# Sliding attention's first pairs between the halves of the query chunks, and a split closing of the feed-forward layers

## The reference

```python
def squared_relu_mlp(h, w1, w2):
    a = jax.nn.relu(h @ w1)
    return (a * a) @ w2

def swiglu(x, w_in, w_out):
    gate, up = jnp.split(x @ w_in, 2, axis=-1)
    return (jax.nn.silu(gate) * up) @ w_out

# second layer of the second block (16 query heads, 4 key heads, head size 64, window 128)
q = rotary((hn @ swa_w_q[j]).reshape(B, S, SWA_Q_HEADS, HEAD_DIM), pos)
# sliding_window_sink_attention: per head
s = q @ k.T * 64 ** -0.5, where seen (the last 128 keys)
p = softmax(concatenate([s, sink]))[..., :-1]
o = p @ v
h = h + o.reshape(B, S, ...) @ swa_w_o[j]
h = h + 0.5 * swiglu(rms_norm(h, ffn2_norm), ffn2_w_in, ffn2_w_out)
```

## Time and profile before

| | us |
|---|---|
| median of 3 runs (1851.13 to 1851.97) | 1851.37 |
| the profiled execution's own time | 1850.78 |
| its span | 1849.0 |
| TensorE busy (matmuls) | 1798.1 |
| VectorE busy | 1152.1 |
| ScalarE busy | 859.8 |
| GpSimd busy | 73.4 |

### The profile page before, as it was taken

One profiled execution on the slowest core, in us unless ns is written; L12 is line 12 of the kernel. 1 busy time (PEld: TensorE's weight loads), 2 busy tenths in 40 slices (PEclk: granted clock), 3 DMA queues, 4 the chain that ended last, 5 costly groups with the idle time before them and its releaser, 6 DMA issues.

```text
span 1849.0 us, 26480 instructions
## 1 busy us (share of the span) xinstructions
PE 1798.1 (97%) x10832; PEld 1567.4 (85%) x10835; DVE 1152.1 (62%) x1149; ACT 859.8 (47%) x1046; POOL 73.4 (4%) x118
## 2 busy tenths in 40 slices
PE   9999999999999999999999999999999999899998
PEld 8989988888989878887888898888888887678886
DVE  7665465557556465556666644666666666766665
ACT  6535455555555455545333454533353344454342
POOL 1000000000220000000000011000000000110000
PEclk9999999999999999999999999999999999999999
DMA  9426355556556355555555544555555554336552
GB/s 316 165 69 206 114 183 204 182 181 192 173 167 193 114 169 196 181 182 171 196 180 192 165 136 137 171 189 197 184 173 193 188 180 154 114 115 205 182 182 90
DMA packets 224327, 318.12 MB, mean 172 GB/s; under 512 B 5585, under 2 KB 194145, under 8 KB 224242
## 3 DMA queue, kind: packets, MB, share of 16 engines
q1 hardware_dynamic: 219442, 300.96, 49.1%
q0 software_dynamic: 4800, 15.94, 2.8%
HBM read 315.83 MB, written 1.05 MB: 171 GB/s over the span
## 4 chain that ended last, share of the span: by engine, by line
PE 90%; DVE 5%; ACT 3%; issue 1%; POOL 0%; DMA 0%; SPq 0%; DVEq 0%; ACTq 0%
PE Y L1702 28%; PE C L1640 21%; PE C L1641 11%; PE C L1670 11%; PE Y L1670 8%; PE Y L1611 3%; DVE w_lo L1072 1%; DVE xn L1113 1%; ACT xn L663 1%; ACT w_hi L648 1%; PE C L2108 1%; PE C L1956 1%; PE C L1750 1%; PE C L1864 1%; PE Y L2087 1%
## 5 line engine op out<-in xcount | busy, mean ns | idle before, releaser
L1072 DVE TENSOR_TENSOR w_lo<-raw,w_hi 128x2048 fp32r<-128x2048 f32 x282 | 645.7, 2291 | 337.4 <-ACT w_hi L648 337.0
L648 ACT ACTIVATE w_hi<-raw 128x2048 fp32r<-128x2048 f32 x282 | 538.4, 1910 | 250.7 <-PE Y L1702 170.9
L1640 PE MATMUL C<-at_hl,w_hi 128*128 128x512 f32 x1440 | 511.3, 398 | 0.0
L1641 PE MATMUL C<-at_hl,w_lo 128*128 128x256 f32 x1440 | 404.2, 281 | 0.0
L1640 PEld LDWEIGHTS C<-at_hl,w_hi 128*128 128x128 f32 x1440 | 270.6, 188 | 66.2
L1641 PEld LDWEIGHTS C<-at_hl,w_lo 128*128 128x128 f32 x1440 | 272.0, 189 | 2.1
L1702 PE MATMUL Y<-w_hi,hid_h 128*128 128x512 f32 x656 | 205.0, 394 | 9.6 <-DVE hid_l L1254 3.8
L1702 PE MATMUL Y<-w_lo,hid_h 128*128 128x512 f32 x656 | 203.2, 391 | 0.0
L1702 PE MATMUL Y<-w_hi,hid_l 128*128 128x512 f32 x656 | 202.2, 389 | 0.0
L1702 PEld LDWEIGHTS Y<-w_hi,hid_h 128*128 128x128 f32 x656 | 117.3, 188 | 35.6 <-DVE hid_l L1254 5.5
L1702 PEld LDWEIGHTS Y<-w_lo,hid_h 128*128 128x128 f32 x656 | 123.1, 188 | 27.4
(11 more groups left out here) (285 smaller groups left out, 2430.7 us busy)
## 6 DMA issues: line engine op xcount, KB each, us to landing
raw<-in_ffn_w_in SPq DMA_DIRECT2D x88, 1024.0 KB, 5.1
raw<-in_w_ff SPq DMA_DIRECT2D x64, 1024.0 KB, 5.8
raw<-in_ffn_w_out SPq DMA_DIRECT2D x44, 1024.0 KB, 4.9
raw<-in_w_mem_kv SPq DMA_DIRECT2D x16, 1024.0 KB, 5.3
raw<-in_w_qkv SPq DMA_DIRECT2D x12, 1024.0 KB, 5.3
raw<-in_sb_w_qkv SPq DMA_DIRECT2D x12, 1024.0 KB, 5.1
raw<-in_w_in_ab SPq DMA_DIRECT2D x8, 1024.0 KB, 10.7
raw<-in_w_mem_q SPq DMA_DIRECT2D x8, 1024.0 KB, 5.4
```

Of the source, the lines that this page charges most:

```text
L648: nc.scalar.activation(w_hi[:, n % RING, :], raw[:, n % RAW, :], ACT.Copy).then_inc(hi_split, 1)
L1072: V.tensor_tensor(w_lo[:, n % RING, :], raw[:, n % RAW, :], w_hi[:, n % RING, :].bitcast(f32), ALU.subtract).then_inc(lo_split, 1)
L1640: mm(tiles(to, 2), wh[:, k, part], hl[:, k, :, :], start=k == 0, stop=False)
L1641: last = mm(to[:, S:2 * S], wl[:, k, part], hl[:, k, 0, :], start=False, stop=k == KT - 1)
```

## The change

Four things.

1. On TensorE the scores of pairs 0 to 4, the transposes of pairs 0 to 2 and the contexts of pair 0 move into `q_cols`, between halves of the query chunks. The chunks go to banks 0 and 1 of `Y` in turn, and so do the turns, so that `C` is free for scores and transposes. In `pairs`, iteration i is scores i, transposes i-2, contexts i-4 (it was i-3).
2. On VectorE `q_cols` has both splits of weight chunks first, then rotations, maxima, shares and copies of the first pairs; in `pairs` the copies stand ahead of the shares of the next pair, the low halves of contexts come one iteration later, and the split of the second output chunk moves from `q_cols` to behind the last copies.
3. On ScalarE the exponentials of pairs 0 to 3 move ahead of the copies of query chunks 2 and 3, and the splits of the first output chunks come earlier.
4. In both feed-forward layers the closing is split: of the last but one `down`, block 1 goes in two halves of 6 matmuls, one ahead of the wait for the last hidden columns and one behind block 0 of the last `down`.

```diff
@@ ScalarE
+            def q_cols_(to, at):
+                n = at.chunk
+                for i in range(4):
+                    if i >= 2:
+                        exps("swa", 2 * i - 4, at)
+                        if i == 3:
+                            exps("swa", 3, at)
+                    else:
+                        hi(n + i + AHEAD)
+                    if i == 2:
+                        exps("swa", 1, at)
+                    act.wait_ge(chunk_done, n + i + 1)
+                    nc.scalar.activation(to[i], tiles(Y[:, i % 2, :], 2), ACT.Copy).then_inc(cols_copied, 1)
+                    if 1 <= i <= 2:
+                        hi(n + i + 1 + AHEAD)
@@ VectorE
             def pairs(at):
-                for i in range(PAIRS + 4):
+                for i in range(4, PAIRS + 5):
                     if i < PAIRS:
                         maxima("swa", i, at, score_bank)
-                    if 1 <= i <= PAIRS:
+                    if i < PAIRS + 2:
+                        probs_out(i - 2, at)
+                    if i == 4:
+                        rope_(qT, 3, at.rot - 4, 1)
+                    elif i <= PAIRS:
                         shares("swa", i - 1, at)
-                    if 2 <= i < PAIRS + 2:
-                        probs_out(i - 2, at)
-                    if i >= 4:
-                        contexts(i - 4, at, "swa")
+                    if i == PAIRS + 1:
+                        lo(at.chunk - 1 + AHEAD)
+                    if i >= 5:
+                        contexts(i - 5, at, "swa")
...
-            def q_cols_(n, at):
-                for i in range(n):
-                    lo(at.chunk + i + AHEAD)
-                    if i >= 1:
-                        rope_(qT, i - 1, at.rot)
-                rope_(qT, n - 1, at.rot)
+            def q_cols_(at):
+                n = at.chunk
                 dve.wait_ge(sink_ready, 1)
+                lo(n + AHEAD)
+                lo(n + 1 + AHEAD)
+                rope_(qT, 0, at.rot, 0)
+                maxima("swa", 0, at, score_bank)
+                lo(n + 2 + AHEAD)
+                shares("swa", 0, at)
+                rope_(qT, 1, at.rot, 1)
+                maxima("swa", 1, at, score_bank)
+                shares("swa", 1, at)
+                maxima("swa", 2, at, score_bank)
+                probs_out(0, at)
+                shares("swa", 2, at)
+                rope_(qT, 2, at.rot, 0)
+                maxima("swa", 3, at, score_bank)
+                probs_out(1, at)
+                shares("swa", 3, at)
@@ TensorE, row_chunk: "for k in parts", with parts=range(2) by default;
@@ relu_ff (and swiglu with N_GLU)
-                for b in range(TB):
-                    for j in (N_REL - 2, N_REL - 1):
-                        down(j, None, [b])
+                down(N_REL - 2, None, [0])
+                down(N_REL - 2, None, [1], [0])
+                down(N_REL - 1, None, [0])
+                down(N_REL - 2, None, [1], [1])
+                down(N_REL - 1, None, [1])
@@ TensorE, attention
+            def pair_scores(p, at, turned_q):
+                if p >= 2:
+                    pe.wait_ge(scores_scaled, at.head + 2 * p - 2)
+                pe.wait_ge(rotated, turned_q + p // 2 + 1)
+                scores("swa", p, at, score_bank)
+            def pair_context(p, at, turned_q):
+                pe.wait_ge(probs_copied, at.head + 2 * p + 2)
+                if p < 2:
+                    pe.wait_ge(rotated, turned_q + 3 + p)
+                elif p >= 6:
+                    pe.wait_ge(scores_scaled, at.head + 2 * PAIRS)
+                else:
+                    pe.wait_ge(ctx_lo, at.ctx + p - 1)
+                context(p, ctx_bank("pair", p), lambda h: h // 4, probs_used)
             def pairs(at):
+                turned_q = at.rot - 4
+                for i in range(5, PAIRS + 4):
                     if i < PAIRS:
+                        pair_scores(i, at, turned_q)
+                    if i < PAIRS + 2:
                         turns(i - 2, at)
+                    pair_context(i - 4, at, turned_q)
                 pe.wait_ge(ctx_lo, at.ctx + 6)
+            def q_cols_(at):
+                def q_part(i, some):
+                    if i >= 2 and 0 in some:
+                        pe.wait_ge(rotated, at.rot + i - 1)
+                    col_chunk(at.chunk + i, "T", at_h, at_l, Y[:, i % 2, :], split=at.turned - 4 if i == 0 else None, some=some)
+                def q_turn(i):
+                    pe.wait_ge(cols_copied, at.copied + i + 1)
+                    rope_(qT, i, i % 2)
+                q_part(0, range(2))
+                q_part(1, [0])
+                q_turn(0)
+                q_part(1, [1])
+                pair_scores(0, at, at.rot)
+                q_part(2, [0])
+                q_turn(1)
+                pair_scores(1, at, at.rot)
+                q_part(2, [1])
+                pair_scores(2, at, at.rot)
+                turns(0, at)
+                q_part(3, [0])
+                q_turn(2)
+                pair_scores(3, at, at.rot)
+                turns(1, at)
+                q_part(3, [1])
+                pair_scores(4, at, at.rot)
+                turns(2, at)
+                pair_context(0, at, at.rot)
+                q_turn(3)
```

More of the change, by code:

```diff
@@ L912, in exps @@
                     last.then_inc(probs_ready, 1)
+            def q_cols_(to, at):
[13 more added lines that the diff above has]
+                        hi(n + i + 1 + AHEAD)
             def pairs(at):
-                for i in range(PAIRS + 3):
+                for i in range(4, PAIRS + 4):
                     if i < PAIRS:
                         exps("swa", i, at)
-                    if i >= 3:
-                        contexts(i - 3, at, "swa")
+                    contexts(i - 4, at, "swa")
             def softplus(p):
@@ L1030, in _ @@
                     post(at, behind)
-                elif s[0] in ("cols", "q_cols"):
+                elif s[0] == "cols":
                     cols(s[1], s[2], at)
+                elif s[0] == "q_cols":
+                    q_cols_(s[2], at)
                 elif s[0] == "kv_cols":
@@ L1691, in col_halves, with row_chunk @@
                 last.then_inc(chunk_done, 1)
-            def row_chunk(n, h, l, first, end, t=None, blocks=range(TB)):
+            def row_chunk(n, h, l, first, end, t=None, blocks=range(TB), parts=range(2)):
                 split_ready(n, t)
@@ L1697, in row_chunk @@
                 for b in blocks:
-                    for k in range(2):
+                    for k in parts:
                         part = slice(b * P, (b + 1) * P)
@@ L1703, in row_chunk @@
                                           start=first and k == 0 and j == 0, stop=end and k == 1 and j == 2)
-                    if b == 1:
+                    if b == 1 and 1 in parts:
                         last.then_inc(chunk_done, 1)
@@ L1776, in up, with down @@
                     pair_chunk(n + 2 * j - 1, at_hl, j % 2, t)
-                def down(j, t=None, blocks=range(TB)):
+                def down(j, t=None, blocks=range(TB), parts=range(2)):
                     pe.wait_ge(hid_lo, at.hid + j + 1 if t is None else t * 3 + (at.hid + j + 1))
                     end = j == N_REL - 1
-                    row_chunk(n + 2 * N_REL - 1 if end else n + 2 * j + 2, *hidden(j % 3), t is None and j == 0, end, t, blocks)
+                    row_chunk(n + 2 * N_REL - 1 if end else n + 2 * j + 2, *hidden(j % 3), t is None and j == 0, end, t, blocks, parts)
                 if same:
@@ L1814, in gate_up, with down @@
                     pair_chunk(n + 3 * j, hl, 1, t)
-                def down(j, t=None, blocks=range(TB)):
+                def down(j, t=None, blocks=range(TB), parts=range(2)):
                     pe.wait_ge(hid_lo, at.hid + j + 1 if t is None else t * 2 + (at.hid + j + 1))
                     end = j == N_GLU - 1
-                    row_chunk(n + 3 * N_GLU - 1 if end else n + 3 * j + 4, *hidden(j % 2), t is None and j == 0, end, t, blocks)
+                    row_chunk(n + 3 * N_GLU - 1 if end else n + 3 * j + 4, *hidden(j % 2), t is None and j == 0, end, t, blocks, parts)
                 split = at.turned - 4
@@ L1846, in swiglu @@
                         down(j)
-                for b in range(TB):
-                    for j in (N_GLU - 2, N_GLU - 1):
-                        down(j, None, [b])
+                down(N_GLU - 2, None, [0])
+                down(N_GLU - 2, None, [1], [0])
+                down(N_GLU - 1, None, [0])
+                down(N_GLU - 2, None, [1], [1])
+                down(N_GLU - 1, None, [1])
             def half_of(t, h):
@@ L1914, in context @@
                             last.then_inc(used, 1)
+            def pair_scores(p, at, turned_q):
[12 more added lines that the diff above has]
+                context(p, ctx_bank("pair", p), lambda h: h // 4, probs_used)
             def pairs(at):
-                h0 = at.head
```

(11 more changed lines are left out.)

10 lines of the change are left out of this document (1 added, 9 removed).

## The result

The changed kernel takes 1858.03 us (median of 7 runs, 1855.73 to 1858.95), the kernel before 1851.23 us (7 runs, 1850.36 to 1851.97): 1.0035 of the time of before, 95% interval 1.0026 to 1.0044. It is slower by 6.8 us, and 1.0 us beyond the range of the prediction.

A forecast was written before the change was run, and what follows sets the result against it. TensorE, busy for 97% of the span, was taken to bound the kernel. From the profiled 1850.78 us, -4.35 + 3.6 + 1.8 gave 1851.8, and 0.6 more for the median 1852.4; range 1847.3 to 1857.0.

The forecast's parts named there:

- Part 1, closings: Six feed-forward closings: layer's last matmul ends 1.2 to 1.36 us earlier; sum -4.35 us, bounds -3 and -7.6.
- Part 2, the chain inside the query columns: VectorE's serial order of the first pairs in the query columns: maxima 0 end at 1585.6, shares 4 start at 1611.50.
- the port term: The +1.8 us of Two engines on one memory.
- Two engines on one memory: VectorE's two-SBUF-input instructions and GpSimd's scaling delay each other in the first pairs: +1.8 us, bounds 0 and +2.8.
- The loop: Sliding-attention pairs: copies before the next pair's shares close a loop, 4.72 us a turn; +3.6 us with the moved split.
- The moved split: VectorE's split of the second output chunk, behind the last copies, delays the output rows by 2.2 us.
- A, forecast, no further clock drop: Pairs' loop: waits for scaling stay at 3.1 us and less, no further clock drop; 1852.4 us; chance 0.42.
- Rival B: Clock falls inside the pairs' loop, 1611 to 1633; each drop +1.6 or +1.7 us: one 1854.1, two 1855.8; chance 0.30.
- C: Pairs' loop: the context wait doesn't bind, turn 3.72 us; 1848.4 us, or 1846.6 without port waits; chance 0.16.
- D: Feed-forward closings: all six give everything, 7.6 us; 1849.1 us; chance 0.12.

The follow-up runs named there:

- closing only: The kernel before with only the split closing of the feed-forward layers (part 4 of the change): 1847.50 us, ratio 0.9979.
- Rotation first: Changed kernel with shares ahead of the previous pair's copies, output chunk split behind context 5, rotations 1 and 2 ahead of shares 0 and 2: 1842.45 us.
- pairs only: The changed kernel with the old closing of the feed-forward layers, so only sliding attention reordered: 1861.53 us, ratio 1.0059.
- kept warm: The changed kernel with 8 matmuls of zeros on TensorE ahead of each pair's transposes in the pairs' loop: 1853.48 us, ratio 1.0013.
- Both cuts: The changed kernel with VectorE's shares ahead of the previous pair's copies, 1848.18 us; or with TensorE's contexts i-4 ahead of transposes i-2, 1849.79 us.
- split later: The changed kernel with VectorE's split of the second output chunk moved behind the low half of context 5: 1856.47 us, ratio 1.0024.
- context first: The changed kernel with TensorE's contexts of pair i-4 ahead of the transposes of pair i-2: 1849.79 us, ratio 0.9992.

## Why the prediction was wrong

It named the mechanism and missed the size: 1852.4 forecast, 1858.03 measured, 1857.0 the upper end. By its own steps:

- **Part 1, closings**, forecast -4.35: right, site by site (4.5 in the profile of after and 4.3 in that of closing only, where the clock takes 0.5 back in the pairs; 3.7 by the medians). The sum of it has 1.36 - 1.22 = 0.12 where it is 0.14, which changes nothing. Also right that the two SwiGLU layers ahead of a block-by-block norm give 0.3 us each and the second ReLU layer nothing.
- **Part 2, the chain inside the query columns**: right. In the times of before less 4.08, shares 4 was forecast for 1607.4 without port waits; it stands at 1609.0, 1.6 us later, where the port term said +1.8. VectorE's waits for the exponentials ahead of shares 1 to 3 are 2.03, 1.09 and 1.15 us, 4.3 together, for about 5.
- **Two engines on one memory**, +1.8: in keeping with these 1.6 us, though no run has the term by itself. Rotation first shows the cause: take the scaling from beside the rotation and both durations go back. The rule of the Trainium skill (SBUF — State Buffer, "Who interferes with whom") agrees: 1.39 against 0.69 us, and 1.98 against 1.61.
- **The loop**, 4.72 us a turn: 4.82 and 4.83 us at 2.4 GHz in two profiles (pairs only, kept warm). Both cuts of it work, and the turn without the context is 3.63 for a forecast of 3.72.
- **The moved split**, 2.2 us: a little too dear, 1.6 us at the place in split later (1.6 to 2.1 by the medians). At the lower clock contexts 6 and 7 kept TensorE busy for part of it: the row waits 1.42 us in the profile of after and 1.99 in kept warm.
- **The clock**: this is the step that failed. The sum has no term for it, since I took "A, forecast, no further clock drop" as the likeliest case: the waits of the loop (3.1 us) are shorter than the one that stood ahead of the old drop (3.6). In the profile of after the clock fell behind waits of 1.11, 0.51 and 1.41 us, and the granted clock is 0.51 for 14 and again for 10 us. Against the turn of 4.82 us it costs 1.35, 1.34 and 0.72 us in the three turns, and 1.3 us from transposes 7 to the first output row (7.06 us, 5.72 in kept warm): 4.7 us. Kept warm says the same from the other side: with the clock held, the stage is 5.7 us longer than before, for 3.6 + 1.8 = 5.4 forecast, and 4.7 shorter than after. Rival B had the place and the cause, with a chance of 0.30, but a price per drop of one turn (1.6 us), where one fall lasted two turns. The Trainium skill (TensorE: Matmul & The Clock Gate, "HAM oscillation") tells of a loop that starts every turn at half clock because TensorE waits in it. These rows agree in kind; they differ in the wait, since the page has one long wait per turn and here the clock fell behind none above 1.41 us.
- **Rivals C and D**: out. C by context first, D by closing only.

With the clock in the sum, 1851.8 + 4.7 - 0.95 (gained ahead of the change) = 1855.55 for the profiled execution; it took 1855.73. So 3.9 of the 5.6 us by which the median missed the forecast are accounted for. The other 1.7 stay open: the median of the changed kernel lies 2.3 us above its profiled execution, and that of before only 0.6, as the forecast took it. It is 2.3 us again in the second profile (1856.19 and 1858.53).

The profiles show one thing that would do most of it. Around 544 us, ahead of down-projections that the change leaves as they were, TensorE waits 2.18 us in every profile. In seven of the thirteen the clock falls behind this wait, in the other six it doesn't; before and both profiles of the changed kernel are among the six. Here after and split later:

```profile
...
540.00:550.00 10.00, 7.82 (x46) 5.74 (x42) 5.81 (x15) 3.86 (x10) 2.70 (x4) 1.00 0.51 171
...
540.00:550.00 10.00, 7.82 (x38) 5.94 (x35) 6.46 (x15) 4.27 (x11) 2.71 (x4) 0.83 0.48 151
...
```

Between the first two closings a profile with this fall alone takes 1.2 to 1.6 us longer than one without. Whether most of the other executions of the changed kernel have this fall isn't shown: they have no trace, and their mean granted clocks (0.990 to 0.992, the profiled one 0.991) are given too coarsely to tell.

## What to carry to other kernels

Moving a copy ahead of the shares looked like taking work off a queue's head; it closed a ring over four engines. Before swapping two calls on an in-order engine, follow each from its result back to itself: if the path passes the same engine once per iteration, its length is the least that the period can be, whatever the engines' own work is. And when TensorE is left partly idle over tens of microseconds, price a rival in which its work there runs at the lower clock for several turns, in the ring above all: here that was 4.7 us, nearly half of what the stage lost.

## What the runs showed of the hardware that was not expected

- No single long wait stood ahead of the fall in the loop: it came at about 1607.1, behind waits of 1.11, 0.51 and 1.41 us. One wait of 2.18 us, around 544 us, was followed by a fall in seven of thirteen profiles and by none in six.
- In the loop the clock stayed at 1.2 GHz for 14 us, with TensorE busy for 10.1 of them by its slowed matmuls (at 2.4 GHz the window of pairs only has 7.1 of 14). It then rose for about three microseconds, most of which TensorE stood idle, and fell for 10 more.
- Eight small matmuls of zeros in each wait held the clock at 1.00 through the same loop. The turn is 4.83 us with them and 4.82 without, both at 2.4 GHz, so they cost nothing that shows.
- The episodes in the pairs are no fixed property of a kernel: the changed kernel's two profiles have different ones, and closing only has a long one in the old pairs stage (0.50 over 10 us) where the same code in the profile of before has a short one. The one behind the second ReLU layer is fixed: it came with the split closing in ten profiles of ten, where the wait ahead of it grew from 0.71 to 2.00 us, and cost nothing.
